# A two-layer hybrid backbone on one Trainium2 core: the signal's short convolution in the block before, and the Hyena tables asked for at the start

## The reference

```
def short_conv(u, w, b):                      # three taps, one token of padding on each side
    out = b
    for j in range(3):
        out = out + up[:, j:j + L] * w[j]
    return out

def hyena_mixer(u, ...):
    u = short_conv(u, conv_w, conv_b)
    x1, x2, v = jnp.split(u, 3, axis=-1)      # two gates and the signal
    z = x1 * long_conv(v, kf[:, 0], bias[0])
    return x2 * long_conv(z, kf[:, 1], bias[1])
```

## Time and profile before

| | |
|---|---|
| time, median of 3 | 3949.2 us |
| lowest and highest | 3948.46, 3953.78 us |
| the profiled execution's own time | 3948.27 us |
| its span, first to last instruction | 3946.4 us |
| mean granted clock of TensorE in it | 0.946 |
| PE busy | 3643.4 us (92%) |
| DVE busy | 2129.9 us (54%) |
| ACT busy | 1417.4 us (36%) |
| POOL busy | 1366.5 us (35%) |
| q1, moved in all | 212.38 MB |
| q0, moved in all | 46.01 MB |

### The profile page before, as it was taken

How to read it: one execution, slowest core, us unless ns; L and a number is a source line. 1 busy time by engine, 2 the same in 40 slices (tenths; PEclk the granted TensorE clock), 3 DMA queues, 4 the chain that set the end, 5 groups by cost and what they waited for, 6 DMA issues and landing times. The chain is left out here.

```text
span 3946.4 us, 53247 instructions
## 1 busy us (share of the span) xinstructions
PE 3643.4 (92%) x19584; PEld 3058.6 (78%) x19584; DVE 2129.9 (54%) x3793; ACT 1417.4 (36%) x2845; POOL 1366.5 (35%) x1239
## 2 busy tenths in 40 slices
PE   7989997999779899999999899969996989999997
PEld 3668996777667688888888679958886768888886
DVE  5468435666676444444444583356676555544544
ACT  3341125666513522222222412246672252222222
POOL 1121122555100055454554421126630005544554
PEclk8989977999889999999999899879998999999999
DMA  5245201001324111111111162010014311111111
GB/s 206 104 168 186 82 4 41 12 8 40 122 78 163 43 43 32 32 43 43 43 32 32 69 202 79 4 39 10 6 39 165 150 43 50 52 48 43 53 52 49
DMA packets 153895, 266.96 MB, mean 68 GB/s; under 512 B 8968, under 2 KB 122777, under 8 KB 151290
## 3 DMA queue, kind: packets, MB, share of 16 engines
q1 hardware_dynamic: 143452, 212.38, 16.2%
q0 software_dynamic: 6352, 46.01, 3.0%
q10 hardware_dynamic: 3920, 6.29, 0.5%
HBM read 229.10 MB, written 33.59 MB: 67 GB/s over the span
## 5 line engine op out<-in xcount | busy, mean ns | idle before, releaser
L2990 POOL TENSOR_TENSOR x<-x,mlp_tmp 128x512 f32<-128x512 f32 x576 | 785.3, 1394 | 1323.7 <-DVE mlp_tmp L2971 1318.5
L2971 DVE TENSOR_TENSOR mlp_tmp<-psum,gate 128x512 f32<-128x512 f32 x576 | 391.7, 689 | 273.1 <-POOL x L2990 194.5
L152 PE MATMUL psum<-act_hi,w_hi 128*128 128x512 f32 (+1 forms) x1280 | 472.6, 369 | 14.4 <-DVE w_lo L2949 14.4
L153 PE MATMUL psum<-act_lo,w_hi 128*128 128x512 f32 (+1 forms) x1280 | 472.3, 369 | 0.0
L154 PE MATMUL psum<-act_hi,w_lo 128*128 128x512 f32 (+1 forms) x1280 | 472.1, 369 | 0.0
L152 PE MATMUL psum<-w_hi,hidden_hi 128*128 128x512 f32 x1152 | 449.9, 391 | 0.0
L153 PE MATMUL psum<-w_lo,hidden_hi 128*128 128x512 f32 x1152 | 448.5, 389 | 0.0
L154 PE MATMUL psum<-w_hi,hidden_lo 128*128 128x512 f32 x1152 | 448.3, 389 | 0.0
L2963 DVE TENSOR_TENSOR hidden_lo<-square,hidden_hi 128x512 fp32r<-128x512 f32 x160 | 102.3, 639 | 591.9 <-ACT hidden_hi L2935 591.9
L1923 DVE TENSOR_REDUCE att_max<-psum 128x1 f32<-128x512 f32 (+2 forms) x272 | 217.4, 799 | 259.7 <-PE psum L154 259.5
L2927 ACT ACTIVATE relu<-psum 128x512 f32<-128x512 f32 x160 | 88.8, 555 | 666.0 <-PE psum L154 666.0
(11 more groups left out here) (386 smaller groups left out, 8238.6 us busy)
## 6 DMA issues: line engine op xcount, KB each, us to landing
w_raw<-in_mlp_w SPq DMA_DIRECT2D x128, 512.0 KB, 3.8
side_w<-in_w_ada SPq DMA_DIRECT2D x40, 1024.0 KB, 6.5
w_raw<-in_w_in SPq DMA_DIRECT2D x32, 512.0 KB, 4.8
hy_ahead<-in_hy_ahead POOLq DMA_DIRECT2D x8, 2048.0 KB, 12.6
open_tab<-in_hy_ahead POOLq DMA_DIRECT2D x8, 1024.0 KB, 13.0
spec_scratch<-open_staged SPq DMA_DIRECT2D x16, 512.0 KB, 2.7
hy_spec<-spec_scratch SPq DMA_DIRECT2D x16, 512.0 KB, 3.5
hy_back<-in_hy_back POOLq DMA_DIRECT2D x2, 4096.0 KB, 29.9
```

Of the source, the lines that this page charges most:

```text
L152: pe.matmul(out, lhs[0], rhs[0], start=start, stop=False)
L153: pe.matmul(out, lhs[0], rhs[1], start=False, stop=False)
L2971: dve.tensor_tensor(tmp[:, j % 2, :], ps[:, 4 + j % 4, :], gate[:, int(t >= LAT_TILES), 512 * h:512 * h + 512], ALU.mult).then_inc(gated.s ...
L2990: pool.tensor_tensor(a, a, tmp[:, j % 2, :], ALU.add).then_inc(added.sem, 1)
```

## The change

- ACT's loop of the latent block gets the first tap of the signal's convolution at `j == n_units + 2`, behind the last `out` but one; DVE gets the other two taps behind its loop. The result goes to the same place as before.
- `hyena_first_loads` sets the two columns of padding of the signal's rows itself, ahead of their load (two memsets, and a wait for them).
- In the Hyena block the convolution of V is gone from ACT and DVE. PE's first turn no longer waits for it. The four `turn_hi` and `turn_lo` stand ahead of X1's convolution.
- POOL's wait ahead of the three forward tables is gone, so all tables are asked for at the block's start. The padding of V is no longer set there.

```diff
@@ phase_latent @@
+    hy_z, v_in = kit.at("hy_z0", [P, 2, SEQ], 96), kit.at("hy_in", [P, 2, SEQ + 2], 16)
...
                 if j < n_units:
                     exp(j)
+                if j == n_units + 2:
+                    act.wait_ge(v_halo.sem, v_halo[0])
+                    act.wait_ge(v_got.sem, v_got[0])
+                    for ct in range(2):
+                        w = kit.hy_conv[:, 4 + ct, :]
+                        act.activation(hy_z[:, ct, :], v_in[:, ct, 0:SEQ], ACT.Identity, scale=w[:, 0:1],
+                                       bias=w[:, 3:4]).then_inc(v_begun.sem, 1)
...
                     invert((j - 3) // 2)
+            for ct in range(2):
+                out, u, w = hy_z[:, ct, :], v_in[:, ct, :], kit.hy_conv[:, 4 + ct, :]
+                dve.wait_ge(v_begun.sem, v_begun[ct])
+                link(dve, dve.scalar_tensor_tensor(out=out, in0=u[:, 1:SEQ + 1], scalar=w[:, 1:2], in1=out, op0=ALU.mult, op1=ALU.add))
+                dve.scalar_tensor_tensor(out=out, in0=u[:, 2:SEQ + 2], scalar=w[:, 2:3], in1=out,
+                                         op0=ALU.mult, op1=ALU.add).then_inc(v_conved.sem, 1)
@@ hyena_first_loads @@
+    pool.memset(v_in[:, :, 0:1], 0.0)
+    pool.memset(v_in[:, :, SEQ + 1:SEQ + 2], 0.0).then_inc(kit.sig("hy_halo").sem, 1)
+    pool.wait_ge(kit.sig("hy_halo").sem, kit.sig("hy_halo").total)
     pool.dma_start(v_in[:, :, 1:SEQ + 1], v_rows).then_inc(kit.sig("hy_v_got", 16, fresh=True).sem, 16)
@@ phase_hyena @@
-    u_in = {(0, V): kit.at("hy_in", [P, 2, SEQ + 2], 16), (0, X1): kit.at("hy_in", [P, 2, SEQ + 2], 184.25),
+    u_in = {(0, X1): kit.at("hy_in", [P, 2, SEQ + 2], 184.25),
...
-    convs = [(0, V), (0, X1)] + ([(1, V), (1, X1), (1, X2)] if context_too else []) + [(0, X2)]
+    convs = [(0, X1)] + ([(1, V), (1, X1), (1, X2)] if context_too else []) + [(0, X2)]
@@ phase_hyena, PE, in turn() @@
                 if o:
                     pe.wait_ge(z_out.sem, z_out[(s, 0, (1, 1 if s else 2 * m // K[s]))])
-                else:
+                elif s:
                     pe.wait_ge(conved.sem, conved[((s, V), 1)])
@@ phase_hyena, ACT @@
+            for m in range(4):
+                turn_hi(0, 0, m)
             act.wait_ge(halo.sem, halo[0])
             for ct in range(2):
-                conv((0, V), ct)
-            for ct in range(2):
                 conv((0, X1), ct)
-            for m in range(4):
-                turn_hi(0, 0, m)
@@ phase_hyena, POOL @@
                 pool.dma_start(behind[1][:], io["hy_back1"]).then_inc(ctx_in.sem, 16)
-            pool.wait_ge(conved.sem, conved[((0, V), 1)])
             for kt in (1, 2, 3):
@@ phase_hyena, DVE @@
-            for ct in range(2):
-                conv((0, V), ct)
+            for m in range(4):
+                turn_lo(0, 0, m)
             for ct in range(2):
                 conv((0, X1), ct)
-            for m in range(4):
-                turn_lo(0, 0, m)
```

More of the change, by code:

```diff
@@ L1683, in phase_latent @@
         stored[s].plan([p for p in range(PAIRS) if p % 2 == s])
+    hy_z, v_in = kit.at("hy_z0", [P, 2, SEQ], 96), kit.at("hy_in", [P, 2, SEQ + 2], 16)
+    v_got, v_halo, v_begun, v_conved = (kit.sig("hy_v_got", 16, fresh=True), kit.sig("hy_halo"), kit.sig("hy_conv_begun"),
+                                        kit.sig("hy_conved"))
+    v_got.plan(range(1))
+    v_halo.plan(range(1))
+    v_begun.plan(range(2))
+    v_conved.plan(range(2))
     def weights_free(p):
@@ L2163, in phase_hyena @@
     invs = [(ct, par) for par in range(2) for ct in range(2)]
-    got = {key: kit.sig(f"hy_got{i}" if i else "hy_v_got", 16) for i, key in enumerate(u_in)}
+    got = {key: kit.sig(f"hy_got{i + 1}", 16) for i, key in enumerate(u_in)}
     for sg in got.values():
```

## The result

The changed kernel takes 3968.58 us (median of 5 runs, 3964.62 to 3971.37) against 3949.2 us before. The ratio on record is 1.0045, 95% interval 1.0031 to 1.0059; the quotient of the two medians is 1.0049. It is slower by about 0.45%, more than the 0.2% that a measurement here tells from no change. The profiled execution took 3968.58 us itself, with a span of 3966.7 us (3946.4 before) and a mean granted clock of 0.943 (0.946). So 20.3 us of span are to be accounted for.

What follows compares the result with a forecast made beforehand. PE works nearly throughout, so only its waits in the Hyena blocks, for DVE and DMA landings, can shrink. 3948.3 us for the profiled execution, + 10 in layer 0 + 2 in layer 1 = 3960, range 3943 to 3971.

Steps and rivals of the forecast that it cites:

- rival C: Both Hyena blocks: gate's row held to 3003 in layer 1, context rows to 1097; +14 + 8, 3970 us; chance 0.1.
- Layer 0, the mechanism: Layer 0's Hyena block: early tables delay the last context row from 1067.3 to near 1092.5, so DVE's products run late; +10 us.
- the working with pairs: Layer 0's DMA queues: context rows alternate with table packets, some 24 pairs at 0.6 to 0.65 us, 8 at 1.3.
- The upper bound of +14: Layer 0's worst case: everything has landed by 1097.5 in any case, which gives +14 us.
- Layer 1: Layer 1's Hyena block: gate's row lands at 2988 to 2997, second spectrum holds L2488 until 3014.3; +2 us, bounds 0 and +8.
- Part 2, turns off the path: Hyena block's start: early turns let PE's first forward step start 10 us sooner, but the first products wait for convolutions.
- Part 3, the last byte: Hyena block's table loads: DMA engines have no room, so asking earlier changes the order; last byte lands within 1 us of before.
- the 1.5 us given as a sign: Sign in both layers' Hyena blocks: the inverse table lands within 1.5 us of its old landing.
- Part 1, the block's end: Latent block's end: ACT's convolution delays layer 0 by 0.6 us, layer 1 by nothing; DVE's taps cost nothing.
- Rival B: DMA queues alternate in bundles, so context rows land at 1077, products start at 1080; no change, 3951 us; chance 0.22.
- "equal within every stretch": DMA queues: the two queues' packet counts are equal within every stretch read, which fits single steps better than bundles.
- Rival A: Both Hyena blocks: rows not held up, tables land earlier; 14 us faster, 3934 us; chance 0.16.

Runs made afterwards that it cites:

- rows_first: changed kernel, but POOL waits for the last row the first products need before asking for the forward and inverse tables; 3944.01 us, ratio 0.9988.
- small_pieces: changed kernel, tables still asked for at once, each of the three forward tables in four transfers of 4 KB per partition instead of one of 16 KB; 3946.88 us.
- split_alone: changed kernel, tables still asked for at once, only the inverse table split into two transfers, first quarter and rest; 3948.09 us, ratio 0.9999.
- turns_behind: changed kernel with the turns' high and low parts put back behind X1's convolution on ACT and DVE; 3967.12 us, ratio 1.0048.
- late_turns_split: changed kernel with tables waiting for the needed rows, inverse table in two transfers, and turns back behind the gate's convolution; 3947.32 us, ratio 0.9994.
- no_taps: changed kernel with tables waiting for the needed rows, and DVE's two taps of the signal's convolution left out; 3943.37 us, ratio 0.9984.
- norms_first: changed kernel, tables waiting for rows, inverse table in two transfers, DVE's second channel tile waiting for POOL's last latent norm; 3932.64 us, ratio 0.9957.
- gate_x1: changed kernel, but POOL waits for the gate's row alone before asking for the big tables, in both layers; 3951.68 us, ratio 1.0002.
- before_split: kernel before the change with only the inverse table split into two transfers, first quarter and rest; 3945.99 us, ratio 0.9987.

## Why the prediction was right

The forecast was slower, 3960 us, with a range of 3943 to 3971; it is 3968.58. The direction and its mechanism were right and are shown; the size was not hit as well: 11.7 us were forecast and 19.4 came, outside the forecast's own range of 3955 to 3966. The time lies near rival C's 3970, but not for rival C's reasons. Point by point:

- **Layer 0, the mechanism.** Shown. It gave the context's last row 35.1 us behind the start, measured 36.2; the products at 37.8, measured 38.7; the second products at 48.5, measured 48.1; the chain 9.4 us late behind the start, measured 9.0. Some of that closeness is luck: the tables' first 16 KB piece came 7.9 us behind the start (8.4 in the forecast), and from there to the row's landing it took 28.3 us, where the working with pairs gives 25 to 26 and its own landing at 1092.5 needs 26.7. The upper bound of +14 is also a microsecond short by the rule given for it (1097.5 less 1092.5, on top of 10). rows_first, small_pieces and split_alone change only what stands beside the rows, and move the products by 9 to 20 us.
- **Layer 1.** The gate's row was to land at 2988 to 2997, 9 to 18 us behind the start; it took 15.0. The second spectrum was to hold L2488 until 35.4 us, measured 36.0. +2 was forecast, +2.4 came in the chain and +1.9 up to the scaling. One wait was not foreseen: X2's late row stands ahead of the first high copy on ACT, and DVE waited 4.48 us for it at L2519. It cost nothing, as the spectrum was not there sooner.
- **Part 2, turns off the path.** Right, by turns_behind. It holds only for the changed kernel: late_turns_split puts the same turns at 11.4 us.
- **Part 3, the last byte.** "Within 1 us" holds for the second spectrum, 40.1 us behind the start against 40.5. The inverse table itself landed 36.0 us behind the start instead of 40.3, at 1095.3, 1.7 us sooner than the old 1097.03; in layer 1 it landed 35.0 us behind the start instead of 37.0. Both are a little more than the 1.5 us given as a sign. The tables' and rows' bytes were the same and their order was not.
- **Part 1, the block's end.** This term was mis-sized: 0.6 us and 0 were forecast, 1.75 and 1.4 measured. ACT's share was right (0.65 and 0, by no_taps). DVE's taps, put at nothing since the block waits for its store, slowed POOL's last norm, and the store waits for that. norms_first takes the share away.
- **What is missing.** 3968.6 less 3960 is 8.6 us. 2.5 of it are the block ends just named, 7.1 the clock (0.8 + 4.7 + 1.6), 0.3 was rounded off the sum, and the blocks came 1.4 us under the forecast: -0.4 in layer 0 and -1.0 in layer 1, where part was given back. Whether the clock's part belongs to the change is not settled. In rows_first and gate_x1 the distance to before also grew by 3 to 5 us in layer 0's second half, in turns_behind and split_alone it did not, with no edit that would explain it. Between the same instructions in 2512 to 2900 of the kernel before, where no run has an edit, the distance changed by between -6.5 us (no_taps) and +3.6 us (turns_behind). The profiled execution of rows_first was the slowest of its ten, 3951.84 us at a granted clock of 0.944, and most of the others had 0.946 to 0.948, so there it is scatter between executions. But all five executions of the change had 0.943 or 0.944, and the fastest was still 15.4 us above the median before, where the two blocks and their block ends account for 13.2, so some of the clock's part probably comes back each time.
- **The rivals.** Rival B (bundles of as many pieces as a transfer has) would have had the products at 1080 and the spectrum's wait as before; they began at 1098.03. The Trainium skill, DMA: Bandwidth & Descriptors, section Queues, rings and completion order, has an engine drain a packet of typically 9 to 17 descriptors before it turns to the next row. The traces do not agree as far as these two queues go: 48 and 48, 113 and 111, 49 and 50, and with small pieces 359 and 357. The prediction's "equal within every stretch" leaves one out: in 2988 to 2989 of the kernel before, q0 has 22 and q1 119, because q1 was still alone at its start; in 2988.4 to 2989, with the tables moving, it is 12 and 13. Rival A (the rows slip through) is near what rows_first makes true by a wait: even then the gain was 0.1%, not the 14 us it gave, since the inverse table's landing took the place of the waits. Rival C gave the time best and was wrong in what it said: the gate's row landed 15.0 us behind layer 1's start and not at its 3003, 24 us behind; the context's last row came 36.2 us behind layer 0's start and not 39.6; and the two blocks cost 10.0 us and not 22.

## What to carry to other kernels

Before a large load is asked for earlier, look at which small transfers are still under way on another queue: while both have work they go piece for piece, so let the large load wait for them or cut it into small pieces, and split it where its first user needs only a part. A head start for an engine pays only up to the last landing that its chain needs; the same reordering was worth next to nothing and 11 us in two versions that differ in their transfers. Work in an engine's shadow is free only if it doesn't slow the engine whose end is waited for.

## What the runs showed of the hardware

- DVE's scalar_tensor_tensor and POOL's tensor_tensor, both with all their operands in SBUF, hold each other up: 0.72 to 1.59 us for POOL and 1.28 to 1.75 us for DVE when they overlap. The Trainium skill, SBUF — State Buffer, section Who interferes with whom, says that a DVE instruction with two SBUF inputs contends with a GpSimd instruction that reads SBUF, and that the later one blocks until the first is done. The trace agrees: in rows_first DVE's first tap began at 1054.86 and ended at 1056.61; POOL's norm that began at 1055.60, with 0.72 us of work to do behind that end, would be through at 1057.33, and ended at 1057.19, 0.14 us sooner (spans on POOL are rough).
- A transfer's time to landing can depend on the piece size of another queue more than on its own bytes: 512 KB of spectrum took 37.1 us beside 16 and 32 KB pieces, 29.0 us where the last ones were 2 KB, and 12.8 us where it had gone ahead of them. In split_alone, with the same 2 KB pieces, it still took 36.7 us in layer 0; there the rows ahead of it in its own queue were late too (the context's last landed 27.3 us behind the start, in before_split 10.4).
- In layer 1 the gate's row landed 15.0 us behind the start after the change, but 10.7 in turns_behind and 10.6 in split_alone, with the same issues in the same order up to then. The DMA records of the traces show the difference: the tables' first 16 KB piece moved 3.3 us behind the start after the change, when 52 of the row's 256 pieces had begun, and 4.2 and 4.5 us behind it in the other two, when 138 and 166 had. The pieces still to come then alternate with the tables'. Why the tables set out sooner in the one is open.
